# A two-layer decoder step whose mixers are reordered: scan levels, gate products and turns between the input projections

## The reference

```python
mod = silu(c) @ mod_w[l] + mod_b[l]              # 6 x 1024 values a row, adaLN
h = rmsnorm(x, norm1_g[l]) * (1 + sc1) + sh1
xa, ga, qb, fb, ib, gb = split(h @ w_in[l])      # 1024 x 3072
xc = causal_conv(xa, conv0)
r, i = sigmoid(xc @ wa + ba), sigmoid(xc @ wx + bx)          # block diagonal
log_a = -8 * softplus(-lam) * r;  a = exp(log_a)
mult = sqrt(-expm1(2 * log_a));  h_t = a_t * h_{t-1} + mult * (i * xc)
yA = rmsnorm(h_t * gelu(ga), rg_out_g[l])
f = lb + (1 - lb) * sigmoid(fb);  q = silu(qb);  k = 1 - f;  v = ib
S_t = f_t * S_{t-1} + k_t v_t^T;  o_t = q_t S_t              # 4 heads of 128 x 128
yB = rmsnorm(o, hg_norm_g) * silu(gb)
x = x + gt1 * (concat(yA, yB) @ w_out[l])
x = x + gt2 * (swiglu or top-2-of-8 MoE)(rmsnorm(x) * (1 + sc2) + sh2)
```

## Time and profile before

| what | value |
|---|---|
| median of 3 runs | 1612.51 us (1612.36 to 1615.31) |
| the profiled execution's own time | 1612.94 us |
| its span from first to last instruction | 1611.2 us |
| PE, DVE, ACT, POOL busy | 94%, 69%, 50%, 2% of the span |
| mean granted clock of TensorE | 0.951 of 2.4 GHz |

### The profile page before, as it was taken

One profiled execution on the slowest core, in us unless ns is written; L12 is line 12 of the kernel. 1 busy time (PEld: TensorE's weight loads), 2 busy tenths in 40 slices (PEclk: granted clock), 3 DMA queues, 4 the chain that ended last, 5 costly groups with the idle time before them and its releaser, 6 DMA issues.

```text
span 1611.2 us, 22232 instructions
## 1 busy us (share of the span) xinstructions
PE 1519.5 (94%) x8633; PEld 1283.0 (80%) x8633; DVE 1104.1 (69%) x1370; ACT 800.1 (50%) x782; POOL 30.7 (2%) x41
## 2 busy tenths in 40 slices
PE   7997898899999977888999999999999999999997
PEld 4785777899997856777788888888888888888885
DVE  2447923455444469316898888888888889888895
ACT  3232322344431423222666667666666666666764
POOL 1002000000000011000000000000000000000000
PEclk7998999899999988895999999999999999999999
DMA  9847695365553375343879979989799797997960
GB/s 305 286 131 235 224 290 161 118 190 178 164 185 129 131 235 184 91 168 121 296 272 350 387 258 394 333 308 394 266 374 376 265 393 272 369 379 261 395 244 27
DMA packets 259170, 408.30 MB, mean 253 GB/s; under 512 B 9784, under 2 KB 151808, under 8 KB 259104
## 3 DMA queue, kind: packets, MB, share of 16 engines
q1 hardware_dynamic: 243552, 396.67, 70.5%
q10 hardware_dynamic: 15552, 10.74, 2.1%
HBM read 401.49 MB, written 5.95 MB: 253 GB/s over the span
## 4 chain that ended last, share of the span: by engine, by line
PE 86%; DVE 9%; ACT 2%; issue 1%; SPq 1%; DMA 0%; ACTq 0%; DVEq 0%
PE ps L694 19%; PE ps L696 19%; PE ps L695 19%; PE ps L574 11%; PE ps L683 4%; PE ps L773 3%; PE ps L830 2%; PE ps L525 1%; PE ps L823 1%; DVE AT L1426 1%; PE ps L652 1%; PE ps L660 1%; PE ps L510 1%; DVE ar L1445 1%; DVE ar L1446 1%
## 5 line engine op out<-in xcount | busy, mean ns | idle before, releaser
L1544 DVE TENSOR_TENSOR slab_lo<-ring,slab_hi 128x2048 fp32r<-128x2048 f32 x264 | 604.6, 2291 | 96.1 <-ACT slab_hi L1161 94.6
L1161 ACT CAST slab_hi<-ring 128x2048 fp32r<-128x2048 f32 x261 | 497.9, 1908 | 154.1 <-PE ps L696 154.1
L694 PE MATMUL ps<-slab_hi,tokens_hi 128*128 128x512 f32 (+1 forms) x768 | 301.4, 392 | 2.0 <-DVE slab_lo L1544 2.0
L696 PE MATMUL ps<-slab_hi,tokens_lo 128*128 128x512 f32 (+1 forms) x768 | 288.6, 376 | 0.0
L695 PE MATMUL ps<-slab_lo,tokens_hi 128*128 128x512 f32 (+1 forms) x768 | 287.0, 374 | 0.0
L574 PE MATMUL ps<-hT,ring 128*128 128x264 f32 x768 | 176.4, 393 | 6.4 <-DVE hT L1296 6.4
L574 PEld LDWEIGHTS ps<-hT,ring 128*128 128x128 f32 x768 | 148.8, 194 | 33.4 <-issue 6.9
L694 PEld LDWEIGHTS ps<-slab_hi,tokens_hi 128*128 128x128 f32 x768 | 145.1, 189 | 27.0 <-DVE slab_lo L1544 2.4
L696 PEld LDWEIGHTS ps<-slab_hi,tokens_lo 128*128 128x128 f32 x768 | 144.8, 189 | 26.3
L695 PEld LDWEIGHTS ps<-slab_lo,tokens_hi 128*128 128x128 f32 x768 | 145.2, 189 | 25.6
L1494 DVE TENSOR_TENSOR slab_lo<-ring,slab_hi 128x2048 fp32r<-128x2048 f32 (+1 forms) x34 | 75.7, 2229 | 104.1 <-ACT slab_hi L1102 104.1
(11 more groups left out here) (318 smaller groups left out, 2041.6 us busy)
## 6 DMA issues: line engine op xcount, KB each, us to landing
ring<-in_moe_w SPq DMA_DIRECT2D x264, 1024.0 KB, 6.8
ring<-in_mod_w SPq DMA_DIRECT2D x48, 1024.0 KB, 5.3
ring<-in_ffn_w SPq DMA_DIRECT2D x30, 1024.0 KB, 5.3
ring<-in_w_in SPq DMA_DIRECT2D x24, 1024.0 KB, 6.1
ring<-in_w_out SPq DMA_DIRECT2D x8, 1024.0 KB, 5.5
out_new_S_sample<-S ACTq DMA_DIRECT2D x2, 2048.0 KB, 14.2
ring<-in_ffn_w SPq DMA_DIRECT2D x4, 768.0 KB, 4.5
uT<-in_x_prompt SPq DMA_DIRECT2D x1, 1024.0 KB
```

Source lines behind the costliest of these rows:

```text
L694: mm(out, x, w, start=start, stop=False)
L696: return mm(out, xl, w, start=False, stop=stop)
L1161: cp(wH[t % 3][:, :], w).then_inc(s_hi, 1)
L1544: tt(wL[t % 3][:, :], w, wH[t % 3][:, :].bitcast(fp32), ALU.subtract).then_inc(s_lo, 1)
```

## The change

- All levels, the gate products and the turns of v are placed between the tiles of the input projections (LEVEL_AFTER, GATES_AFTER, V_AFTER), and the parts of ACT and DVE that belong to them with them (EXP_AFTER and the rest). Tiles use three banks in place of four, and the gates three in place of two. The GELU gate's group goes ahead of v's.
- The multiplier is computed as sqrt(-(a^2 + 1) tanh(log a)), with a square on ACT (L1046 of the new kernel), in place of a reciprocal of 1 - tanh on DVE.
- Modulation slabs after the first eight run in fours: four slabs side by side in the four strips of one bank, one copy, and one turn with two matmuls of 36 columns. A mixer has six such fours in layer 0 and four in layer 1, all after the last tile. Four slots of the ring come free at once. The vectors are added to their bias in 12 or 8 small DVE operations in place of one.
- v times k for the samples is a scaled copy on ACT (four of 128x128 a sample). DVE then updates S in one fused operation a head (four of 128x128 a sample), and POOL does nothing there.
- Scratch moves to other buffers, and S is loaded earlier.

Cut to its core:

```diff
-        xc, rg, ig, ag, mu, gt, g2 = (lot(i) for i in range(7))
-        LD = [ar[:, 1024 * i:1024 * (i + 1)] for i in range(2)]
-        LW = [ar[:, 2048 + 1024 * i:3072 + 1024 * i] for i in range(2)]
-        keT = ar[:, 4096:5120].rearrange("p (t h d) -> p t h d", t=2, h=H)
-        ke = ar[:, 5120:6144].rearrange("p (h t) -> p h t", h=H)
-        vbk = ar[:, 6144:6656].rearrange("p (g e) -> p g e", e=P)
+        xc, rg, ig, mu, g2 = (lot(i) for i in range(5))
...
-            for l in range(L):
-                pool.wait_ge(s_S, 16 * (l + 1))
-                pool.wait_ge(s_f, l + 1)
-                fb = fs.rearrange("p h b -> p b h")
-                for b in range(NS):
-                    ins = g.tensor_tensor(out=S[:, b * H:(b + 1) * H, :], in0=S[:, b * H:(b + 1) * H, :],
-                                          in1=wide(fb[:, b, :], P), op=ALU.mult)
-                ins.then_inc(s_S1, 1)
...
+            def project_four():
+
+                n = mods[0]
+                w = [slab()[:, 0:2048].rearrange("p (k n) -> p k n", k=KC) for _ in range(4)]
+                pe.wait_ge(s_mev, n)
+                for k in range(KC):
+                    for j in range(4):
+                        last = mm(ps[7][j * STRIP:(j + 1) * STRIP, 0:256], cond_flat[:, k * COND:k * COND + STRIP],
+                                  w[j][:, k, :], start=(k == 0), stop=(k == KC - 1))
+                last.then_inc(used, 4)
+                mods[0] += 4
+                if mods[1] < n:
+                    turn_four()
...
+                for c in range(2):
+                    last = mm(out[:, c, :], modrow[:, n // 4 % 2, c * P:(c + 1) * P], picks[:, :],
+                              start=True, stop=True)
+                last.then_inc(s_mtr, 4)
...
+            def level(l, v):
+                pe.wait_ge(s_lw, (LEVELS + 1) * l + v + 1)
+                if v >= 2:
+                    pe.wait_ge(s_lc, (LEVELS + 1) * l + v - 1)
+                if v == 3:
+                    pe.wait_ge(s_tg, 8 * (l + 1))
+                lw = LW[v % 2].rearrange("p (h t) -> p h t", h=H)
+                if v == LEVELS:
+                    for h in range(H):
+                        last = mm(ps[2][:, h * P:(h + 1) * P], lw[:, h, 0:P], lw[:, h, P:T], start=True, stop=True)
+                else:
+                    for t in range(2):
+                        for h in range(H):
+                            kk = lw[:, h, t * P:(t + 1) * P] if v else FB[:, h, t * P:(t + 1) * P]
+                            qq = lw[:, h, t * P:(t + 1) * P] if v else QB[:, h, t * P:(t + 1) * P]
+                            last = mm(ps[2 + 2 * (v % 2) + t][:, h * P:(h + 1) * P], kk, qq, start=True, stop=True)
+                last.then_inc(s_lp, 1)
+
+            def gates(l):
+                pe.wait_ge(s_xc, l + 1)
+                pe.wait_ge(s_gw, 64 * (l + 1))
+                pe.wait_ge(s_lc, (LEVELS + 1) * l + 2)
+                for i in range(8):
+                    if i >= 3:
+                        pe.wait_ge(s_tg, 8 * l + i - 2)
+                    mm(ps[GATE_BANKS[i % 3]][:, 0:N], gw[:, i % 2, i // 2, :], xc[:, i // 2, :],
+                       start=True, stop=True).then_inc(s_gp, 1)
+
             def layer(l):
+                for j in range(U):
+                    if j % 2 == 0:
                         w = slab()[:, 0:SLAB].rearrange("p (k n) -> p k n", k=KC)
...
+                    if j == GATES_AFTER:
+                        gates(l)
+                    if j in LEVEL_AFTER:
+                        level(l, LEVEL_AFTER[j])
+                    if j in V_AFTER:
+                        t = V_AFTER[j]
+                        pe.wait_ge(s_u, U * l + 20)
+                        pe.wait_ge(s_tg, 8 * (l + 1))
+                        pe.wait_ge(s_v, 2 * l + t)
+                        for h in range(H):
+                            last = nc.tensor.transpose(ps[7][:, h * P:(h + 1) * P],
+                                                       IB[:, h, t * P:(t + 1) * P], ident[:])
+                        last.then_inc(s_vp, 1)
...
+                def level_exp(v):
+                    act_.wait_ge(s_ld, LEVELS * l + v)
+                    A(LD[v % 2], LD[v % 2], ACT.Exp).then_inc(s_le, 1)
...
+                            A(mu[:, c, :], rg[:, c, :], ACT.Tanh, scale=coef[:, l, c:c + 1])
...
+                            ins = A(ag[:, c, :], rg[:, c, :], ACT.Exp, scale=coef[:, l, c:c + 1])
+                        ch(ins)
+                        A(g2, ag, ACT.Square).then_inc(s_a, 1)
...
+                    if j in EXP_AFTER:
+                        level_exp(EXP_AFTER[j])
+                    if j == ROOT_AFTER:
+                        act_.wait_ge(s_m2, l + 1)
+                        A(mu, mu, ACT.Sqrt, scale=-1.0).then_inc(s_mu, 1)
+                        nc.scalar.preload_act_table_set("exp_and_others")
...
+                for b in range(NS):
+                    act_.wait_ge(s_vb, NS * l + b + 1)
+                    if b >= 2:
+                        act_.wait_ge(s_vbd, NS * l + b - 1)
+                    for h in range(H):
+                        ins = A(vbk[b % 2][:, h, :], ps[2 + b % 2][:, h * P:(h + 1) * P], ACT.Copy,
+                                scale=FB[:, h, T + b:T + b + 1])
+                    ins.then_inc(s_vk, 1)
+                    if b == 0:
+                        act_.wait_ge(s_gb, l + 1)
+                        A(oT[:, 0:2, 0:T], ps[0][:, :].rearrange("p (h t) -> p h t", h=2), ACT.Copy)
+                        A(oT[:, 2:4, 0:T], ps[1][:, :].rearrange("p (h t) -> p h t", h=2), ACT.Copy)
+                    for _ in range(FILL[l][1][b]):
+                        mod_rows_four()
...
+                def level(v):
+                    if v < LEVELS:
+                        dve.wait_ge(s_lw, (LEVELS + 1) * l + v)
...
+                diff(1)
+                dve.wait_ge(s_tq, l + 1)
+                ch(stt(QB, g2, 1.0, QB, ALU.add, ALU.mult))
+                ts(QB, QB, 0.5, None, ALU.mult).then_inc(s_lw, 1)
+                conv(0)
+                conv(1)
+                level(1)
+                conv(2)
+                conv(3)
...
                 dve.wait_ge(s_a, l + 1)
-                ch(ts(g2, mu, -1.0, 1.0, ALU.mult, ALU.add))
-                ch(V.reciprocal(g2, g2))
-                stt(mu, mu, -2.0, g2, ALU.mult, ALU.mult).then_inc(s_m2, 1)
+                stt(mu, g2, 1.0, mu, ALU.add, ALU.mult).then_inc(s_m2, 1)
+                level(4)
...
+                level(7)
+                level(8)
+                take(LEVELS)
+                dve.wait_ge(s_kx, l + 1)
+                tt(ke, ke, FB[:, :, 0:T], ALU.mult).then_inc(s_ke, 1)
+
...
+                dve.wait_ge(s_S, 16 * (l + 1))
+                for b in range(NS):
+                    dve.wait_ge(s_vk, NS * l + b + 1)
                     for h in range(H):
...
-ORDER = (3, 2, 0, 4, 1, 5)
+ORDER = (3, 2, 0, 1, 4, 5)
...
-FILL = ((4, (1,) * 9, (1,) * 8, 2, 1), (3, (1,) * 8 + (0,), (0, 0, 1, 0, 0, 1, 0, 0), 2, 1))
-assert all(a + sum(b) + sum(c) + d + e == MOD_DONE[l + 1] - MOD_DONE[l]
-           for l, (a, b, c, d, e) in enumerate(FILL))
+FILL = ((1, (1, 0, 1, 0, 1, 0, 1, 0), 1), (1, (1, 0, 0, 0, 1, 0, 0, 0), 1))
+assert all(4 * (a + sum(b) + c) == MOD_DONE[l + 1] - MOD_DONE[l] for l, (a, b, c) in enumerate(FILL))
+U_BANKS = (0, 1, 6)
+GATE_BANKS = (4, 5, 7)
+GATES_AFTER = 12
+LEVEL_AFTER = {9: 0, 11: 1, 13: 2, 14: 3, 15: 4, 17: 5, 18: 6, 20: 7, 21: 8}
+V_AFTER = {19: 0, 20: 1}
+EXP_AFTER = {9: 1, 10: 2, 12: 3, 13: 4, 14: 5, 16: 6, 18: 7, 19: 8}
+ROOT_AFTER = 14
+GELU_AFTER = 15
+KE_AFTER = 18
 
 W_IN = (MOD_DONE[0], MOD_DONE[1] + 16 + 34)
 W_OUT = tuple(W_IN[l] + 12 + MOD_DONE[l + 1] - MOD_DONE[l] for l in range(2))

```

373 lines of the change are left out of this document (179 added, 194 removed).

## The result

The changed kernel takes 1584.89 us (median of 4 runs, 1584.35 to 1586.58), the kernel before 1613.12 (4 runs, 1612.36 to 1615.31). The ratio is 0.9829, 95% interval 0.9814 to 0.9844: 28.2 us less, where the forecast was 42.4 less: inside the stated range (1555 to 1590), but above the forecast's own band (1560 to 1579). The profiled execution of the changed kernel is 1584.35 us, its span 1582.6.

What follows compares the result with a forecast made beforehand. PE, busy 94%, was taken to bound the kernel, with a chain through DVE bounding each mixer's second half. Mixers at -19.2 and -23.2 us, together -42.4 from 1612.9, gave 1570.5, forecast as 1570; range 1555 to 1590.

Steps and rivals of the forecast that it cites:

- supply and stalls: Rival: slabs at the mean rate (10 us) and more waits per mixer at levels 2 to 7; 1580 to 1588, chance 0.26.
- the wait ahead of the gates: First stretch: PE waits about 3.8 us because DVE still holds the banks that the gates use.
- level 5: First stretch: PE reaches this level before DVE is done behind the gates; a wait of 1.5 us with handoffs.
- the cover that the prediction named: First stretch: DVE's other levels end 3 to 4 us before PE asks; slower DVE behind the gates shows above that.
- edits at no cost: Reciprocal (6.75 us) out, square on ACT in, and small edits: on no path PE waits for, except in the DVE sum.
- The argument for 4.3: Modulation four: same 32 matmuls as four old slabs of 1.07 us, which already run in four strips, so 4.3 us.
- Its clock stays at the low level: Second stretch's tail, from the last four to handoffs: 14.7 us, at the old low clock, head norm 3.9.
- The term of 1.8 us: Second stretch, first mixer: late slabs for single fours add 1.8 us, at 387 GB/s and 2.7 us a slab.
- a wait of over 5 us in all: Sign that the forecast is wrong: fours waiting for their slabs more than 5 us in all.
- the store now is issued about as far ahead of the projection as before: Layer 0's output projection: the store of S costs nothing new; that stage and the rest move along unchanged.
- The clock rival: Rival: waits drop PE to the low clock from the gates to the last tile, +50 us per mixer; 1657, chance 0.04.

Runs made afterwards that it cites:

- gates_13: Changed kernel with the gate products issued after tile 13 instead of tile 12; 1584.60 us against 1584.9.
- recip: Changed kernel with the old multiplier put back (reciprocal on DVE, no square on ACT); 1594.13 us against 1584.9.
- half_slabs: Changed kernel with the mixers' modulation slabs loaded by half, PE multiplying as much, outputs meaningless; 1566.74 us against 1584.9.
- wide_rows: Changed kernel with the mixers' modulation weights, same bytes, loaded in rows of 4 KB instead of 1 KB; 1575.32 us against 1584.9.
- split_late: Changed kernel with layer 0's split of the first two FFN slabs moved into the output projection's residual loop; 1570.12 us against 1584.9.
- singles: Changed kernel with only the groups of four undone, each modulation slab projected, copied and turned by itself; 1595.52 us against 1584.9.

## Why the prediction was right, and where its size was wrong

The time lies in the stated range, and the two mechanisms that carry the forecast hold: the levels and gates stand between the tiles at the cost that was worked out, and without the chain through DVE the second stretch went from 109.2 to 68.7 us and from 101.8 to 52.0. Of the 42.4 us 28.2 came, which is the band of the rival "supply and stalls" (0.26), not the forecast's (0.52).

**Tiles.** The first stretch was forecast at 120.2 us and took 120.5, by its terms: the wait ahead of the gates 3.87 (3.8 forecast), the gates 6.64 (7.2), level 5 2.29 (1.5), levels 1.95 each (2.03). That the sum was hit to 0.3 us is partly luck. From start to start a level costs 1.8 us, which makes 1.9 less in eight and a half, and the gates cost 0.6 less; against that the clock behind level 5's wait, which had no term, takes 1.8 more (level 5 and the tile behind it are 7.1 us long where others are 5.35), and the wait itself 0.8. gates_13 and recip confirm the cover that the prediction named: DVE sets the pace from the gates to level 5. The recip run also corrects the "edits at no cost": the reciprocal's going was counted inside the DVE sum, and is worth 9.2 of the 28.2 us.

**Fours.** A group was taken at 4.3 us with 3.4 as the lower bound; it takes 3.66 at the full clock, 0.64 less for each. The argument for 4.3, that a single slab's matmuls lie in strips as well, was wrong in size: eight in a chain took 1.07, 32 take 3.66 and not 4.28. Part of that is the end of each chain: from start to start it is 3.59 against four times 1.01.

**The tail.** "Its clock stays at the low level" was half right: the last group ran at 5.56 us and the head norm behind it at 2.03, not 3.87.

**Supply.** The term of 1.8 us was the first that failed. It took 387 GB/s from the 2 us of the earlier trace rows (and 43 us from 169 on end at 212, not at 217); in the bound stretch the changed kernel moves 351, 3.0 us a slab of 1 MB and not 2.7. Waits came to 8.5 us, and behind two of them a group ran at the low clock (5.61 and 5.56 instead of 3.66): 3.9 us more. half_slabs takes all the waits away, and 9.8 us with them; wide_rows leaves 2.6 us of waits. The stretch as a whole came out only 5.6 us over, because six groups of 3.66 and the head norm at the full clock cost 5.7 less than forecast: here too errors cancel. The prediction named a wait of over 5 us in all as what would make it wrong; the rival "supply and stalls" had 10 us for this, and the time is in its range (1580 to 1588), if not for its second half: behind the gates no level waits but level 5. By its own sign, then, the supply term was wrong.

**The step that failed most** is this sentence: "the store now is issued about as far ahead of the projection as before, so that stage and the rest of the kernel move along unchanged". The first half holds (8.1 us ahead, before 10.4). The second does not: the store lands 22.7 us after its issue instead of 13.8, the two splits that wait for it hold the residuals back, and the projection takes 8.4 us more. split_late shows it: with the splits out of the way, and the store landing no sooner, the projection takes 42.8 us. Why it lands later can be read, but was not isolated: from issue to landing the engines move 4.9 MB in the kernel before (13.8 us at 353 GB/s) and 8.3 MB here (22.7 at 367), 2.1 of them the store's, so that about six slabs are in its way instead of under three. With singles it landed in 18.4 us, with half of the modulation bytes in 20.9.

**Mixer 1** was hit to 2.2 us, with errors that cancel: the fours and the norm came to 2.7 us less than forecast, a fall of the clock in the state rows cost 3.9, small items 0.9 less, and the tiles were 1.9 longer.

Against the span: +0.3 and +5.6 in mixer 0, +8.4 in its projection, +1.9 and +0.3 in mixer 1, and -2.8 in all other stretches and the start make 13.7 of the 13.8 us between forecast and profile.

**The clock rival** (1657) is out: no tile ran at 7 us. The Trainium skill's rule in "TensorE: Matmul & The Clock Gate", section "HAM oscillation — how this bites in real kernels", is borne out only behind single waits: gates 6.64 instead of 3.80, a group 5.6 instead of 3.66, and full clock again after one group. Its example waits for a transfer after every group; here most tiles and levels follow each other without any.

## What to carry to other kernels

When a change shortens a stretch that covers transfers, look up every DMA that ends behind it, stores too: its landing time is no constant, and an instruction that waits for it in a strict queue holds up whatever stands behind it, related or not. Put what overwrites a stored buffer as late in each queue as its own consumer allows. And before gains of separate edits are added, take the granted clock of the untouched stretches out of each: here 5.6 us of it came and went with edits elsewhere.

## What the runs showed of the hardware

- The length of the rows that a transfer reads matters above 1 KB: with all DMA engines busy, slabs of 1 MB moved at 348 to 351 GB/s with rows of 1 KB and at 401 to 421, in most slices, with rows of 4 KB (wide_rows), worth 4.2 us in mixer 0's second stretch. The Trainium skill, "DMA: Bandwidth & Descriptors", section "Specifications", gives 512 B as the least transfer for full rate; these runs do not agree, and the measurement decides.
- 32 matmuls of 256 columns in four column strips take 3.66 us as one group, eight of one slab 1.07: from start to start 3.59 against 4.04 us, 11% less for the same work, and one turn of 0.64 us instead of four of 0.61.
- A PE that is busy by the records can still lose its clock: in a run of state rows (one-column products and broadcasts) it was busy for 12.00 of 12 us and granted 0.50 (changed kernel, 636 to 648 us).
- The same wait does not always cost the same: behind 3.87 us of idle the gates took 6.64 us in the changed kernel and behind 3.85 us 3.80 in singles; within the changed kernel a group took 5.56 us behind 2.09 us and 3.66 behind 2.21. The five runs of singles lie 11.9 us apart.
